# Eight raw-piece buffers for the experts' up stage, and a residual buffer of half the features

## What is computed

```python
def peer_ffn(xn, w_query, sub_keys, expert_down, expert_up):
    ...
    def block(args):
        xb, ib, gb = args
        u = expert_down[ib]
        act = jax.nn.gelu(jnp.einsum('tkd,td->tk', u, xb).astype(f32))
        vv = expert_up[ib]
        return jnp.einsum('tk,tkd->td', (gb * act).astype(vv.dtype), vv)
...
        x = x + peer_ffn(rms_norm_2(x, norm2_g[l]), peer_w_query[l], peer_sub_keys[l], peer_down[l], peer_up[l])
```

## Time and profile before

| what | us |
|---|---|
| median of 3 runs | 3113.21 |
| lowest and highest run | 3112.70 and 3121.73 |
| the profiled execution | 3119.72 |
| its span, first to last instruction | 3117.8 |
| first matmul of the experts' up stage, from the span's start | 2493.8 |
| start of its last matmul | 3111.9 |

### The profile page before, as it was taken

How to read it: one execution, slowest core, us unless ns; L and a number is a source line. 1 busy time by engine, 2 the same in 40 slices (tenths; PEclk the granted TensorE clock), 3 DMA queues, 4 the chain that set the end, 5 groups by cost and what they waited for, 6 DMA issues and landing times.

```text
span 3117.8 us, 49431 instructions
## 1 busy us (share of the span) xinstructions
PE 3076.5 (99%) x15766; PEld 2565.3 (82%) x15766; DVE 1651.3 (53%) x2846; ACT 1667.8 (53%) x2515; POOL 2527.7 (81%) x1980
## 2 busy tenths in 40 slices
PE   9999999999999999999999999999999999999999
PEld 8888888888888887888888888888888877777777
DVE  5468244444310033645722376277762178888888
ACT  5754543334344455544444434477764466776776
POOL 7888889999999998897788889988888877755553
PEclk9999999999999999999999999999999999999999
DMA  6554555555565564454455555555555599988997
GB/s 234 175 169 154 190 180 184 186 183 187 182 205 193 195 200 162 157 188 161 145 173 196 194 178 195 189 179 179 177 180 192 190 327 342 336 318 327 333 345 286
DMA packets 188117, 659.86 MB, mean 212 GB/s; under 512 B 22848, under 2 KB 28096, under 8 KB 187360
## 3 DMA queue, kind: packets, MB, share of 16 engines
q1 hardware_dynamic: 158896, 572.59, 54.2%
q0 software_dynamic: 20480, 67.15, 6.1%
q10 hardware_dynamic: 8624, 18.65, 1.8%
HBM read 649.92 MB, written 8.39 MB: 211 GB/s over the span
## 4 chain that ended last, share of the span: by engine, by line
PE 78%; DMA 8%; DVE 6%; issue 4%; ACT 2%; POOL 1%; SPq 0%; DVEq 0%; POOLq 0%; ACTq 0%
PE ps L2354 30%; PE ps L2358 15%; DMA raw<-in_stream 8%; PE ps L2452 8%; PE ps L2445 8%; PE ps L2447 8%; PE ps L2510 3%; DVE lo_x L2263 2%; ACT ps L1262 1%; POOL lo L582 1%; PE ps L2994 1%; PE ps L2990 1%; PE ps L2995 1%; PE ps L2991 1%; PE ps L2992 1%
## 5 line engine op out<-in xcount | busy, mean ns | idle before, releaser
L582 POOL TENSOR_TENSOR lo<-raw,hi 128x512 fp32r<-128x512 f32 x1656 | 2154.7, 1314 | 334.7 <-PE ps L2358 114.6
L648 ACT ACTIVATE hi<-raw 128x1024 fp32r<-128x1024 f32 x1083 | 1135.9, 1058 | 1023.4 <-PE ps L2358 401.6
L2354 PE MATMUL ps<-xx,hi 128*128 128x512 f32 x4288 | 1526.1, 399 | 6.3 <-DVE xx L1287 6.3
L2358 PE MATMUL ps<-xx,lo 128*128 128x256 f32 x4288 | 1203.3, 281 | 1.4 <-POOL lo L582 1.4
L2354 PEld LDWEIGHTS ps<-xx,hi 128*128 128x128 f32 x4288 | 806.3, 188 | 196.2 <-DVE xx L1287 8.0
L2358 PEld LDWEIGHTS ps<-xx,lo 128*128 128x128 f32 x4288 | 810.5, 189 | 2.5 <-POOL lo L582 2.2
L598 POOL TENSOR_TENSOR lo<-raw,hi 128x512 fp32r<-128x512 f32 x128 | 176.3, 1400 | 120.3 <-ACT hi L648 120.1
L2445 PE MATMUL ps<-hi,xx 128*128 128x512 f32 x608 | 241.1, 397 | 2.1 <-ACT hi L648 1.6
L2447 PE MATMUL ps<-hi,xx 128*128 128x512 f32 x608 | 237.0, 390 | 0.0
L2990 PE MATMUL ps<-hi,hg 128*128 128x512 f32 x508 | 202.0, 398 | 17.3 <-DVE hg L2209 15.5
L612 POOL DMA_INDIRECT row<-in_stream,row_up x128 | 129.2, 1009 | 97.6 <-DVE ps L2275 69.0
(11 more groups left out here) (388 smaller groups left out, 4074.9 us busy)
## 6 DMA issues: line engine op xcount, KB each, us to landing
raw<-in_stream SPq DMA_DIRECT2D x1083, 512.0 KB, 3.3
side_acts<-side ACTq DMA_DIRECT2D x32, 128.0 KB, 2.2
wg<-in_w_gates ACTq DMA_DIRECT2D x1, 2048.0 KB, 9.0
bias<-in_rpb ACTq DMA_DIRECT2D x1, 2048.0 KB, 7.8
gbc<-in_gains ACTq DMA_DIRECT2D x2, 1024.0 KB, 6.0
spill<-hx ACTq DMA_DIRECT2D x4, 512.0 KB, 3.9
hx_end<-spill ACTq DMA_DIRECT2D x1, 2048.0 KB, 8.5
row<-in_stream,row_up POOLq DMA_INDIRECT x128, 7.0
```

Source lines behind the costliest of these rows:

```text
L582: nc.gpsimd.tensor_tensor(lo[:, k % 2, n], raw[:, k, n], hi[:, k, n].bitcast(F32), ALU.subtract)\
L648: nc.scalar.activation(hi[:, k, :], raw[:, k, :], ACT.Copy).then_inc(hi_done, 1)
L2354: M.matmul(ps[:, b_, :], w_h, xx[:, i_].rearrange("p a t -> p (a t)"), start=first, stop=False)
L2358: return M.matmul(t_bank(b_), w_l, xh[:, i_, :], start=False, stop=last)
```

## The change

In the up stage, the raw pieces go through eight buffers: the four of `raw` and four new ones, which take the place of tables that are not needed any more (offset 0), of the upper half of `hx_end` (two), and of `side` (the activations of the 64 tokens, stored just before). Round r uses buffers 0 to 3 when r is even and 4 to 7 when it is odd. SP's loop ends in front of the stage; its 256 loads are written out, each with its own wait: on the `lo` of piece u-8 in place of that of piece u-4. `hx_end` holds 1024 features; its second half is loaded by SP between the loads of piece 200 and 201, once the four stores of the first half, which SP issues behind the load of piece 144, have landed.

```diff
+        raws = [raw[:, k, :] for k in range(4)] + [
+            place(f"raw_up{b}", [P, PIECE], at)[:] for b, at in enumerate(
+                [0, X_AT + 16384, X_AT + 20480, F_AT + 24576])]
+
+        def raw_up(r, k):
+            return raws[(4 * r + k) % 8]
...
-        hx_end = place("hx_end", [P, TT, D], X_AT + 8192)
+        hx_end = place("hx_end", [P, TT, PIECE], X_AT + 8192)
...
-            with sp.Fori(1, ROUNDS) as i:
+            with sp.Fori(1, UP0) as i:
...
-            for n, b in enumerate((0, 1, 2, 3, 6, 4, 7, 5)):
+
+            def up_load(u):
+
+                if u < 4:
+                    sp.wait_ge(lo_done[u], UP0 * 2)
+                elif u == 4:
+                    sp.wait_ge(gated_done, GROUPS)
+                    sp.wait_ge(unit_used, after("peer_down", 2 * (GATE0 + GROUPS // 2) + 8))
+                elif u == 5:
+                    sp.wait_ge(unit_used, after("peer_up", 0))
+                elif u == 7:
+                    for g in range(4):
+                        sp.wait_ge(side_stored[g], 16 * 8)
+                elif u >= 8:
+                    sp.wait_ge(lo_done[u % 4], (UP0 + u // 4 - 2) * 2 + 2)
+                sp.dma_start(raws[u % 8], stream[4 * UP0 + u]).then_inc(loaded_up[u % 8], 16)
...
+            for u in range(4 * UPS):
+                up_load(u)
+                if u == 4 * 36:
+                    for n in range(4):
+                        store(n, n)
+                if u == 4 * 50:
+                    sp.wait_ge(out_stored, 16 * 4)
+                    sp.dma_start(hx_end[:], spill[:, :, PIECE:]).then_inc(got_h2, 16)
+            for n, b in enumerate((6, 4, 7, 5)):
+                store(n + 4, b)
...
-                    nc.gpsimd.tensor_tensor(lo_up(0)[:, n], raw[:, 0, n],
+                    nc.gpsimd.tensor_tensor(lo_up(0)[:, n], raw_up(r, 0)[:, n],
...
+            def up_hi(r, k):
+
+                u = 4 * r + k
+                act.wait_ge(loaded_up[u % 8], 16 * (u // 8 + 1))
+                act.wait_ge(unit_used, after("peer_up", u - 3))
+                nc.scalar.activation(hi[:, k, :], raw_up(r, k), ACT.Copy).then_inc(hi_done, 1)
...
-            act.dma_start(hx_end[:], spill).then_inc(got_h, 16)
+            act.dma_start(hx_end[:], spill[:, :, 0:PIECE]).then_inc(got_h, 16)
...
+            dve.wait_ge(got_h2, 16)
             add_rows_sum(1)
```

More of the change, by code:

```diff
@@ L259, in build @@
         raw_copied = sem("raw_copied")
+        loaded_up = [sem(f"loaded_up{b}") for b in range(8)]
+        got_h2 = sem("got_h2")
         block = ctx.enter_context(nc.Block())
@@ L559, in _, with store @@
                         "a p n -> p (a n)")).then_inc(loaded[k], 16)
-            for n, b in enumerate((0, 1, 2, 3, 6, 4, 7, 5)):
+            def up_load(u):
[12 more added lines that the diff above has]
+                sp.dma_start(raws[u % 8], stream[4 * UP0 + u]).then_inc(loaded_up[u % 8], 16)
+            def store(n, b):
                 tt, c = out_part(b)
@@ L563, in _ @@
                     sp.wait_ge(fin_done, n + half[0] + 1)
-                    f = slice(c * NCH + half[0] * T, c * NCH + half[1] * T)
-                    sp.dma_start(out[tt * P:(tt + 1) * P, f], hx_end[:, tt, f])\
-                        .then_inc(out_stored, 16)
+                    lo_n, hi_n = half[0] * T, half[1] * T
+                    f, v = c * NCH, c % 2 * NCH
+                    sp.dma_start(out[tt * P:(tt + 1) * P, f + lo_n:f + hi_n],
+                                 hx_end[:, tt, v + lo_n:v + hi_n]).then_inc(out_stored, 16)
+            for u in range(4 * UPS):
[8 more added lines that the diff above has]
+                store(n + 4, b)
             sp.wait_ge(out_stored, 16 * 9)
@@ L1244, in _ @@
                         take_hi(r0 + u // 4, u % 4)
-            take_ahead(UP0, 0, 1, 2)
+            def up_hi(r, k):
[3 more added lines that the diff above has]
+                nc.scalar.activation(hi[:, k, :], raw_up(r, k), ACT.Copy).then_inc(hi_done, 1)
+            for k in range(3):
+                up_hi(0, k)
             expert_gelu(127)
-            take_ahead(UP0, 3)
+            up_hi(0, 3)
             side_store(31)
             act.wait_ge(unit_used, after("peer_up", 0))
-            act.dma_start(hx_end[:], spill).then_inc(got_h, 16)
+            act.dma_start(hx_end[:], spill[:, :, 0:PIECE]).then_inc(got_h, 16)
             act.wait_ge(act_gated, 128 - GATE0)
@@ L1261, in raw_copy @@
                         act.wait_ge(lo_done[k_before], 2 * (UP0 + before) + half + 1)
-                    nc.scalar.activation(copy_bank(r, half), raw[:, k, half * NCH:(half + 1) * NCH],
-                                         ACT.Copy).then_inc(raw_copied, 1)
+                    nc.scalar.activation(copy_bank(r, half),
+                                         raw_up(r, k)[:, half * NCH:(half + 1) * NCH], ACT.Copy).then_inc(raw_copied, 1)
             for r in range(1, UPS):
@@ L1268, in _ @@
                 for k in range(4):
-                    take_hi(UP0 + r, k)
+                    up_hi(r, k)
                     if (r, k) in COPIED:
@@ L2258, in up_lo @@
                     n = slice(half * NCH, (half + 1) * NCH)
-                    whole = raw[:, k, n]
+                    whole = raw_up(r, k)[:, n]
                     if (r, k) in COPIED:
@@ L2286, in add_rows_sum @@
                 dve.wait_ge(row_used, QT * (half + 1))
-                v = hx_end[QT:P, 1, half * PIECE:(half + 1) * PIECE]
+                v = hx_end[QT:P, 1, :]
                 link(V.tensor_tensor(v, accum(QT * half)[QT:P], v, ALU.add))
@@ L2293, in add_residual @@
                 tt, c = out_part(b)
-                v = hx_end[:, tt, c * NCH:(c + 1) * NCH]
+                v = hx_end[:, tt, c % 2 * NCH:(c % 2 + 1) * NCH]
                 if tt:
```

## The result

| | before | changed |
|---|---|---|
| median of runs, us | 3117.47 (4 runs) | 3087.98 (4 runs) |
| lowest and highest | 3112.70 and 3122.97 | 3085.20 and 3095.82 |
| span of the profiled execution | 3117.8 | 3093.5 |
| up stage, first to last start of a matmul | 2493.8 to 3111.9: 618.1 | 2489.1 to 3087.5: 598.4 |

The ratio is 0.9917, 95% interval 0.9895 to 0.9939: 26 us or 0.8% faster (19 to 33); the two medians of four runs stand 29.5 us apart. The four later runs of the same kernel have a median of 3094.

A forecast was written before the change was run, and what follows sets the result against it. PE and DMA were both close to full, with PE losing 26 us in the up stage, its stalls rooted in late raw pieces. The sum was 3113.2 - 18.4 + 2.4 + 0 = 3097 us, range 3089 to 3113.

The forecast's parts named there:

- What can be had at most: Up stage: 2560 matmuls need about 592 us of 618.1, so 26 us are lost and 3087 is the least time.
- Part 1: Up stage: loads waiting for u-8 cover GpSimd's lateness, and PE's waits of 18.4 us go.
- short stalls that stay: Up stage: 2.4 us, an eighth, kept as remaining loss (bounds 0 and 10), leaving a gain of 16.0.
- T + 0, T + 2.7, T + 3.8 and T + 3 to 4: From PE's round start T: hi of piece 3, next round's first hi, GpSimd's lo, and hg made.
- Part 2: DMA in the first half: must deliver 356 GB/s, with 360 to 370 taken as what it can give.
- Part 3: Stage start: the 2.0 us stall stays; loads beside the side store cost 2.9 us at worst, taken as 0.
- Part 4: Halved residual: 2.1 MB more traffic in the second half, cost 0; 5.8 us if the cover failed.
- Part 5: SP's 256 written-out loads in place of a loop in the up stage: cost 0.
- Rival C: Five row buffers: gathers starve behind the deep raw queue, 34 us lost in place of 18.4, time 3129; chance 0.09.

The follow-up runs named there:

- traffic run: Changed kernel with half a piece (256 KB) more loaded every round from round 4 on, into a place nothing reads; stage 598.95 us.
- run with the store ahead: Changed kernel with piece 5 of the stage loaded only when the side activations are stored in HBM; stage 595.1 us.
- lead of four: Changed kernel with the load of piece u waiting for the lo of piece u-4 again, eight buffers kept; 3123.7 us, ratio 1.0031.
- third row moved: Kernel before, four buffers, with VectorE adding the third gathered row behind the making of the next round's hg; 3099.22 us, ratio 0.9964.

## Why the prediction was right, point by point

**What can be had at most.** 26 us were given as lost in the stage. The lag of 25.7 at its end is no proof of it, as its 9.256 us a round are nearly the same figure. The sum as written gives (280 - 5.2) / 1186 x 2560 = 593 us, not 592, and undisturbed rounds (36 to 60 of the changed kernel) take 9.227 us, which makes 590.5 for 64: 27.6 us were lost, and 8 still are. So 3087 was not the least possible time. That the runs' gain by the ratio is also 26 us is chance: the stage gave 19.7.

**Part 1, the waits that go.** 18.4 us were to go. The lag from round 4 to the end was 21.1 us before and is -0.6 now, so 21.7 went; the 2.0 us more that the changed kernel has lost by round 4 (6.6 for 4.6) leave the 19.7 of the stage. Two things were sized too small. I kept 2.4 us for short stalls that stay, and hardly any stayed. And I counted 5.52 us of ScalarE's wait at the change of halves as a reason for PE's stall there to stay. That wait is unchanged (5.5 us), yet PE loses nothing at it now: from round 32 to 36 the lag grew 1.9 us before and 0.3 now. The steps foreseen as T + 0, T + 2.7, T + 3.8 and T + 3 to 4 are T + 0.3, T + 3.0, T + 4.1 and T + 4.3 in the second half. For the first half this step was wrong. I gave VectorE 8.14 us a round and had `hg` made ahead of `lo`, or, in eight rounds of 28, beside it and done by T + 7.5. VectorE took 258.0 us for 1168 / 40 = 29.2 rounds, 8.84 a round; `hg` was held up by `lo` in 19 of the 29 rounds from 3 to 31, L2253 still has a maximum of 3234 ns, and `hg` was done as late as T + 9.3. It cost only about 1.5 us, because PE wants it at T + 9.2. That margin was luck, not forecast.

**Part 2, DMA.** The need of 356 GB/s was right (356 from 2530 to 2780, 352 to 2800). The ceiling was set too low, at 360 to 370, from the share of the kernel before; the traffic run puts it at 382 or more. The rate at share 0.93 divided by the share does not give the rate at share 1. By the Trainium skill's "HBM Reference", specification table, a core has 358 GB/s with its neighbour active; 382 over 250 us is above that figure, so it did not bind here, as the windows of the earlier trace rows had said.

**Part 3, the start.** Taken at 0 with an end of 2.9 us; it cost 2.2 us by the store, 3.1 with the slow matmuls behind (the lag at round 2 went from 3.7 to 6.8). The run with the store ahead showed the loads of pieces 5 and 6 as the cause.

**Part 4, the residual.** Nothing with the lead of eight. With the lead of four up to 6.9 us, of which 4.0 + 2.5 stand right behind the transfers, where 5.8 was the price.

**Part 5.** The written-out loads: lead 4 up to round 32 lags as before does, so nothing.

The stage alone makes 19.7 us, with 16 foreseen. The 26 us of the ratio hold some 6 us more, and they were not foreseen. They lie in front of the stage or in the spread of the runs, where the edits change nothing; why the medians there differ by up to 10 us stays open.

**Rival C** didn't occur: in the changed kernel VectorE never waits for a gathered row, though loads may run eight pieces ahead in the other queue. How long a gather takes to land there the profile doesn't give.

## What to carry to other kernels

Add up one turn of a buffer (from "free" through issue, landing and every step that must read it) and set it against the time that the ring gives; at 8.4 of 9.3 us a ring of four lost 20 us, and a lead of one piece more cured it, so try the smallest ring first. When the last waits are on something made late, follow the chain back: the third row, the port and GpSimd's list all stood at the scene; without the gathers of activations nothing was won, with the third row moved 9 us, and with the load earlier all of it. When one wait is gone, look at the busy times again: here VectorE, at 149.9 of 150 us, is what the first half would meet next. Loads that start earlier take the DMA engines from what was alone there; look for the small transfer that someone waits for.

## What the runs showed of the hardware

- The DMA engines moved 382 GB/s over 250 us at a busy share of 1.00, while 356 GB/s already read as a share of 0.97 and 335 as 0.93. The rate divided by the share (367 and 360) was below what could be had.
- A VectorE instruction of 0.68 us with two inputs in SBUF (L2253) took up to 3.23 us beside two GpSimd instructions of 2.55 us together.
- A store of 128 KB took 2.7 us from issue to the end of the wait for it with the 1 MB load of the residual beside it, and 4.95 us with two loads of 512 KB issued on SP's queue as well.
- After a stall of PE of 4.2 us the matmuls ran at the lower clock for about 5 us (granted clock 0.66 from 2500 to 2510), in both executions of the changed kernel. The 2.0 us stall of the kernel before had a stretch of about 3 us behind it, the 2.4 us stall of the store-first run none, so the length of one stall does not settle it.
